# Turning V as 32x32 squares on VectorE, storing it unsplit, and splitting each chunk as it comes back

## The chip, the cores and the metric

The kernel runs on one core of one Trainium2 chip. The metric is the device time of one execution in microseconds, as the median of several executions. Each core has a matrix engine (TensorE, PE in the profile), VectorE (DVE), ScalarE (ACT), GpSimd (POOL) and a queue for DMAs (SyncE, SP). Each engine runs its own instructions in program order, and they meet at semaphores.

## The reference, cut to what matters

One layer works on 2048 tokens of 1024 channels. `x @ w_in` makes all projections; four branches (attention, pooling, a gated recurrence, attention to a memory) are gated, multiplied by `w_branch`, summed, multiplied by `w_out` and normalised. The change lies in the first branch, causal "stick-breaking" attention with 4 heads of 128:

```python
z = jnp.einsum('bhqd,bhnkd->bhqnk', q_blk, k_pre) * scale
log_1m = jnp.where(valid, jax.nn.log_sigmoid(-z), 0.0)
within = jnp.einsum('bhqnk,kj->bhqnj', log_1m, suffix)
later = lax.cumsum(totals, axis=3, reverse=True) - totals
w = jnp.where(valid, jnp.exp(jax.nn.log_sigmoid(z) + within + later[..., None]), 0.0)
o = jnp.einsum('bhqnk,bhnkd->bhqd', w.astype(v.dtype), v_pre)
```

The weight of a key is sigmoid(z) times the product of (1 - sigmoid(z)) over all later keys. So the kernel goes through the keys backwards, with a running product.

## The kernel before, in words

**Precision.** Products are in float32r, as three matmuls: each operand is split into a hi part (a copy rounded to float32r) and a lo part (the difference), and hi·hi + hi·lo + lo·hi is summed (`pass3`, lines 823 to 825).

**Stages.** The tokens are worked in two halves of 1024 (T). In each half `w_in` is applied in 36 pairs of column tiles. A pair is 14 pieces of 6 matmuls of 512 columns (`piece`); sums of blocks on the other engines save one of eight products. The first 8 pairs make Q, K, V and the gate of the four heads. The two pairs of head h+1, and for the last head the first pairs of the merge, are laid as filling between the steps of head h's attention.

**Attention.** For one head, `STEPS` lists steps (chunk c of 512 queries, chunk k of 512 keys, block j of 128 queries): 12 steps a head in the first half and 28 in the second, four to a group with one (c, k). Every engine loops over the same step number s, up to `ns + TAIL`:

- TensorE in step s: `scores(s)` (three matmuls into bank ZZ), then, where s >= 7 and s % 4 == 3, the first half of a group's `values` (W times V), then half pieces of filling, then, where s % 4 == 0, the second half of `values`, and last the transposes `turned(s - TURN)` of the weights of an earlier step, from REST into PSUM (line 949).
- ScalarE in step s: `turned_hi(s - 4)`, the hi copy of turned weights (L1380), then `shares(s)`: two sigmoids of the scores, KEEP (L1366) and SHARE (L1371), then its part of the filling.
- VectorE: `remainder(s - 1)`, a scan of KEEP into REST (L1901), the mask on diagonal steps (L1890), `turned_lo(s - 4)` (L1914) and filling (L1746, L1784).
- GpSimd: `weights(s - 1)`, REST times SHARE in place (L2390), then filling (L2333, L2341, L2320).

In step s = 4i + 7 TensorE starts the values of group i. They read the tile VC, which holds one group's V, hi and lo, in a single buffer.

**How V gets there.** The projection leaves V with channels on partitions. At pieces 10 and 12 of each head's second pair, `turn` lets TensorE transpose it, four 128x128 blocks at a time into a PSUM bank of the projection (L890). ScalarE copies the hi part out (L1277), VectorE subtracts the lo part (L1755), and SyncE stores both to DRAM (`pk_v`, L498). For each group `load_v` reads hi and lo back into VC with one DMA (L518), after the last group's values are done with it.

REST has four slots, one per block j; TURN is 3, so the transposes of step s's weights stand at the end of step s + 3. The first block of the next key chunk takes its start value from the slot of four steps ago.

Of the kernel before, what the change touches and what calls it, by code (L numbers as in the profile page):

```python
# [11 lines left out]
P = 128  # L12
# [70 lines left out]
TURN, TAIL = 3, 5  # L83
# [29 lines left out]
def first_step(half, h):  # L113
    return half * HEADS * NS[0] + h * NS[half]

# [60 lines left out]
def build(nc, xt, xrow, memt, w8, w4, wgate, wpool, prm, cst, ln_g, ln_b, out):  # L176
    with ExitStack() as ctx:
# [24 lines left out]
        B = R + 48.03125  # L202
# [23 lines left out]
        REST = at("REST", R + 32, [BLOCKS, C + 2])  # L226
        WTH = at("WTH", R + 40.03125, [2, BLOCKS, HALF], F32R)
        KC = [at(f"KC{i}", R + 48.03125 + 4 * i, [2, C], F32R) for i in range(2)]
        KEEP = at("KEEP", R + 56.03125, [2, C + 2])
        WTL = at("WTL", R + 60.0625, [2, BLOCKS, HALF], F32R)  # L230
        VC = at("VC", R + 68.0625, [BLOCKS, 2, P], F32R)
# [20 lines left out]
        LR_ = [at(f"LR{i}", R + k, [T]) for i, k in enumerate((28, 8, 52.0625))]  # L252
# [3 lines left out]
        LG = [at(f"LG{i}", R + 52.0625 + 4 * i, [T]) for i in range(2)]  # L256
        LA, LT = at("LA", R + 60.0625, [T]), at("LT", R + 64.0625, [T])
# [38 lines left out]
        pk_v = nc.dram_tensor("pk_v", (HEADS, P, SEQ // P, 2, P), F32).ap()  # L296
# [33 lines left out]
        v_kept = [sem("v_hi_kept"), sem("v_lo_kept")]  # L330
# [3 lines left out]
        v_tr, v_hi, v_blk = sem("v_tr"), sem("v_hi"), sem("v_blk")  # L334
# [122 lines left out]
        def _(sp):  # L457
# [35 lines left out]
            def keep_values(g):  # L493
                half, h = g // PAIRS, g % PAIRS // 2
                hh = half * HEADS + h
                for part, of in ((1, places(half, STL)[1]), (0, places(half, STL)[2])):
                    sp.wait_ge(v_blk, 2 * hh + 2)
                    sp.dma_start(pk_v[h, :, half * TB:(half + 1) * TB, part, :],  # L498
                                 of[:].bitcast(F32).rearrange("p (b m) -> p b m", m=P)).then_inc(v_kept[part], 16)
# [9 lines left out]
            def load_v(half, h, i):  # L509

                n, k = first_group(half, h) + i, STEPS[half][BLOCKS * i][1]
                if i == 0:
                    for kept in v_kept:
                        sp.wait_ge(kept, 16 * (half * HEADS + h + 1))
                    if h == 0:
                        wait_if(sp, o_out[1], 16 * 3 * half)
# [24 lines left out]
            def attention(half, h):  # L541
                ns, fill = NS[half], beside(half, h)
                for g, i in fill[:filled(half, h, -1)]:
                    piece(g, i)
                for s in range(ns + TAIL + 1):
                    if s == ns + 1 and h + 1 == HEADS:
                        sp.wait_ge(z_done, S_END[half])
                        for k in range(2):
                            sp.wait_ge(y_kept, 16 * 2 * (half + 1))
                            sp.dma_start(Y[k][:], pk_y[k]).then_inc(y_back, 16)  # L550
                        load_b(half, 0, 0)
                    if s == 1 and h in (1, 2):
                        sp.wait_ge(y_f, y_count(half, 0, h))
                        sp.dma_start(pk_y[h - 1], Y[h + 1][:]).then_inc(y_kept, 16)
                    if s == 1:
                        load_v(half, h, 0)
                    elif BLOCKS < s <= ns and s % BLOCKS == 0:
                        load_v(half, h, s // BLOCKS - 1)
                    if BLOCKS <= s and s % BLOCKS == 0 and s + BLOCKS < ns:
                        load_k(half, h, s // BLOCKS + 1)  # L560
                    if s in (ns, ns + 1) and h + 1 < HEADS:
                        load_k(half, h + 1, s - ns)
                    if s:
                        for g, i in fill[filled(half, h, s - 2):filled(half, h, s - 1)]:
                            piece(g, i)
# [253 lines left out]
        def _(pe):  # L819
# [16 lines left out]
            def piece(g, i, ks=(0, 1)):  # L836
# [9 lines left out]
                elif i == 0:  # L846
                    pe.wait_ge(a_lo, g + 1)
                    wait_if(pe, ad_done, 4 * (g - 1) + 2)
                    if 2 <= l <= 2 * HEADS and l % 2 == 0:
                        pe.wait_ge(v_blk, 2 * (half * HEADS + l // 2))  # L850
# [30 lines left out]
            def turn(g, part):  # L881

                hh = g // PAIRS * HEADS + g % PAIRS // 2
                v, c = places(g // PAIRS, ST)[2], J[(g + 1) % 2]
                if part:
                    pe.wait_ge(v_blk, 2 * hh + 1)
                else:
                    pe.wait_ge(ad_done, 4 * g + 2)
                for j in range(4):
                    mm = nc.tensor.transpose(c[:, j * P:(j + 1) * P], v[:, (4 * part + j) * P:(4 * part + j + 1) * P],  # L890
                                             IDENT[:])
                mm.then_inc(v_tr, 1)
# [47 lines left out]
            def turned(half, h, s):  # L940

                gs = first_step(half, h) + s
                c, k, j, a, diag, end = STEPS[half][s]
                pe.wait_ge(w_done, gs + 1)
                wait_if(pe, wt_lo, gs - 1)
                n = C - a
                for b in range(n // P):
                    w = REST[:, j, n - P * (b + 1):n - P * b]
                    mm = nc.tensor.transpose(TB_[gs % 2][:, b * P:(b + 1) * P], w, IDENT[:])  # L949
                mm.then_inc(wt_done, 1)  # L950

            def values(half, h, i):
# [6 lines left out]
                pe.wait_ge(v_in, 16 * (n + 1))  # L959
# [182 lines left out]
        def _(act):  # L1142
# [32 lines left out]
            def room(g, p):  # L1175
# [3 lines left out]
                if kind == "head":  # L1179
# [3 lines left out]
                    if i % 2 == 0 and p:  # L1183
                        wait_if(act, v_kept[1], 16 * hh)
                    elif i % 2 == 0 and i:
                        act.wait_ge(sil, half * NB * KB + i // 2)
                    elif i % 2 and p:
                        act.wait_ge(q_kept, 16 * (hh + 1))
                    elif i % 2:
                        wait_if(act, v_kept[0], 16 * hh)  # L1190
                elif kind == "merge" and i >= 2:
                    gates_read(half, n, 2 * i + p - 4)
                elif kind == "merge" and n == 0:
                    if i == 0:
# [3 lines left out]
                        elif half or not p:  # L1198
                            act.wait_ge(k_kept, 32 * HEADS * (half + 1))
                            act.wait_ge(v_kept[1], 16 * HEADS * (half + 1))  # L1200
                        else:
                            act.wait_ge(v_kept[0], 16 * HEADS * (half + 1))
                    elif p:
                        act.wait_ge(w_done, S_END[half])
                    elif half:
                        act.wait_ge(v_kept[0], 16 * HEADS * (half + 1))
# [38 lines left out]
            def piece(g, i):  # L1245
# [24 lines left out]
                if g % PAIRS < 2 * HEADS and g % 2 and i in (10, 12):  # L1270
                    values_hi(g, 0 if i == 10 else 1)

            def values_hi(g, part):

                hh = g // PAIRS * HEADS + g % PAIRS // 2
                act.wait_ge(v_tr, 2 * hh + part + 1)
                nc.scalar.copy(places(g // PAIRS, STL)[2][:, part * C:(part + 1) * C], J[(g + 1) % 2][:]).then_inc(v_hi, 1)  # L1277
# [121 lines left out]
            def attention(half, h):  # L1399
# [8 lines left out]
                for s in range(ns + TAIL + 1):  # L1408
                    if 0 <= s - TURN - 1 < ns:
                        turned_hi(half, h, s - TURN - 1)  # L1410
# [280 lines left out]
        def _(dve):  # L1691
# [56 lines left out]
            def turned(g, part):  # L1748

                hh = g // PAIRS * HEADS + g % PAIRS // 2  # L1750
                t = slice(part * C, (part + 1) * C)
                dve.wait_ge(v_hi, 2 * hh + part + 1)
                dve.wait_ge(k_kept, 32 * (hh + 1))
                hi, lo = places(g // PAIRS, STL)[2], places(g // PAIRS, STL)[1]
                V_.tensor_tensor(lo[:, t], J[(g + 1) % 2][:], hi[:, t].bitcast(F32),  # L1755
                                 ALU.subtract).then_inc(v_blk, 1)
# [30 lines left out]
            def piece(g, i):  # L1787
# [13 lines left out]
                if l < 2 * HEADS and l % 2 and i in (10, 12):  # L1801
                    turned(g, 0 if i == 10 else 1)
# [89 lines left out]
            def remainder(half, h, s):  # L1892
# [4 lines left out]
                n, before = C - a, C - STEPS[half][s - BLOCKS][3]  # L1897
# [3 lines left out]
                V_.tensor_tensor_scan(REST[:, j, 0:n + 1], KEEP[:, gs % 2, 0:n + 1], ZB[gs % 2][:, 0:1].broadcast_to([P, n + 1]),  # L1901
                                      1.0 if diag else REST[:, j, before:before + 1], ALU.mult, ALU.bypass
# [25 lines left out]
            def attention(half, h):  # L1928
# [9 lines left out]
                for s in range(ns + TAIL + 1):  # L1938
# [7 lines left out]
                    if 0 <= s - TURN - 1 < ns:  # L1946
                        turned_lo(half, h, s - TURN - 1)
# [365 lines left out]
        def _(pool):  # L2313
# [69 lines left out]
            def weights(half, h, s):  # L2383
# [5 lines left out]
                w = REST[:, j, 0:n]  # L2389
# [167 lines left out]
```

## Time and profile before

| | |
|---|---|
| median of 3 runs | 2293.91 us (2293.49 to 2294.52) |
| the profiled execution's own time | 2293.96 us |
| its span in the trace | 2292.2 us |
| TensorE matmul busy | 2279.5 us, 99% |
| VectorE, ScalarE, GpSimd busy | 1444.4, 1060.2, 1224.3 us (63%, 46%, 53%) |
| granted TensorE clock | 0.999 of full speed |
| DMA | 297.84 MB, 130 GB/s over the span |

The span runs from the first to the last instruction of the program that was profiled; 1.8 us of the execution lie outside it. Matmuls overlap in the pipeline, so the time of one is read as the distance from its start to the next one's start, not as its duration. The attention of the four heads lies at about 75 to 290 us in the first half and 1150 to 1480 us in the second.

### The profile page before, as it was taken

What the parts mean: (1) busy time and instruction counts of PE and PEld (TensorE: products, weight loads), DVE (VectorE), ACT (ScalarE), POOL (GpSimd) and SP (SyncE); (2) the same over time, 40 slices, a digit from 0 to 9 for tenths busy, and PEclk for the clock granted to TensorE, in tenths of its full rate; (3) what the DMA queues carried; (4) which work ended last, traced back from release to release, by engine and by line L of the source; (5) the groups of instructions that cost most, each with busy time, mean ns of one, the idle gap of its engine ahead of it and who ended that gap; (6) DMA issues with size and microseconds to landing.
All of it is one profiled execution on the core that took longest, in us unless ns stands there. A gap on an engine that the chain in (4) does not pass through costs nothing.

```text
span 2292.2 us, 29991 instructions
## 1 busy us (share of the span) xinstructions
PE 2279.5 (99%) x10824; PEld 1886.8 (82%) x10824; DVE 1444.4 (63%) x1658; ACT 1060.2 (46%) x1627; POOL 1224.3 (53%) x847
## 2 busy tenths in 40 slices
PE   9999999999999999999999999999999999999998
PEld 6888888888878888888888888888888778888887
DVE  7565542764496478568877777733854585486476
ACT  5555542343385255332576676632342583355220
POOL 1666643865456355435476566644863556456341
PEclk9999999999999999999999999999999999999999
DMA  6544422123334345373344543322133334354442
GB/s 234 187 159 158 139 83 97 55 83 129 113 104 133 134 124 148 105 284 138 108 159 139 165 156 124 125 92 78 56 120 124 92 103 134 130 156 132 152 161 83
DMA packets 114419, 297.84 MB, mean 130 GB/s; under 512 B 11232, under 2 KB 41056, under 8 KB 113248
## 3 DMA queue, kind: packets, MB, share of 16 engines
q1 hardware_dynamic: 112544, 290.68, 38.6%
q10 hardware_dynamic: 1728, 5.24, 0.7%
q8 instruction: 87, 1.43, 0.3%
q14 instruction: 60, 0.49, 0.1%
HBM read 216.19 MB, written 71.30 MB: 125 GB/s over the span
## 4 chain that ended last, share of the span: by engine, by line
PE 97%; DVE 1%; DMA 1%; issue 0%; DVEq 0%
PE J L823 21%; PE J L825 21%; PE J L824 21%; PE ZZ L995 8%; PE AO L995 8%; PE ZZ L825 2%; PE ZZ L824 2%; PE ZZ L823 2%; PE AO L825 2%; PE AO L824 2%; PE AO L823 2%; PE AO L949 1%; PE JX L949 1%; PE ZZ L1030 1%; PE JX L825 1%; PE JX L823 1%
## 5 line engine op out<-in xcount | busy, mean ns | idle before, releaser
L2341 POOL TENSOR_TENSOR WLS<-SR,WHS 128x512 fp32r<-128x512 f32 x264 | 414.3, 1588 | 110.1 <-ACT WHS L1161 102.5
L823 PE MATMUL J<-XBH,WHS 128*128 128x512 f32 x1152 | 452.3, 393 | 0.0
L825 PE MATMUL J<-XBH,WLS 128*128 128x512 f32 x1152 | 449.1, 390 | 0.0
L824 PE MATMUL J<-XBL,WHS 128*128 128x512 f32 x1152 | 448.9, 390 | 0.0
L823 PE MATMUL J<-XBH,WH 128*128 128x512 f32 x864 | 340.3, 394 | 0.4 <-DVE WL L1764 0.2
L825 PE MATMUL J<-XBH,WL 128*128 128x512 f32 x864 | 337.0, 390 | 0.0
L824 PE MATMUL J<-XBL,WH 128*128 128x512 f32 x864 | 336.8, 390 | 0.0
L825 PEld LDWEIGHTS J<-XBH,WLS 128*128 128x128 f32 x1152 | 216.2, 188 | 46.0
L824 PEld LDWEIGHTS J<-XBL,WHS 128*128 128x128 f32 x1152 | 216.4, 188 | 43.6 <-issue 0.2
L823 PEld LDWEIGHTS J<-XBH,WHS 128*128 128x128 f32 x1152 | 216.4, 188 | 43.5 <-issue 0.2
L2333 POOL TENSOR_TENSOR SR<-RAW 128x512 f32<-128x512 f32 x71 | 100.6, 1417 | 269.8 <-DMA RAW<-w 230.8
L1746 DVE TENSOR_TENSOR ST<-J,ST 128x512 f32<-128x512 f32 x160 | 109.5, 685 | 209.1 <-PE J L825 162.2
L2390 POOL TENSOR_TENSOR REST<-REST,SHARE 128x512 f32<-128x512 f32 (+3 forms) x160 | 165.6, 1037 | 119.7 <-DVE REST L1901 116.1
L2407 POOL TENSOR_TENSOR BL<-BRAW,BH 128x512 fp32r<-128x512 f32 x64 | 89.3, 1401 | 220.2 <-ACT BH L1429 220.0
L823 PEld LDWEIGHTS J<-XBH,WH 128*128 128x128 f32 x864 | 162.3, 188 | 40.1 <-issue 7.3
L1161 ACT CAST WHS<-SR 128x1024 fp32r<-128x1024 f32 x144 | 151.3, 1051 | 93.5 <-POOL SR L2333 92.4
L825 PEld LDWEIGHTS J<-XBH,WL 128*128 128x128 f32 x864 | 162.2, 188 | 34.8
L824 PEld LDWEIGHTS J<-XBL,WH 128*128 128x128 f32 x864 | 162.3, 188 | 31.8 <-issue 0.2
L2333 POOL TENSOR_TENSOR SR<-SR,RAW 128x512 f32<-128x512 f32 x71 | 105.6, 1488 | 120.4 <-PE J L825 118.4
L1243 ACT COPY ST<-J 128x512 f32<-128x512 f32 x160 | 93.8, 590 | 125.1 <-PE J L825 122.4
L1901 DVE TENSOR_TENSOR_SCAN REST<-KEEP,REST,ZZ 128x513 f32<-128x513 f32 x96 | 122.8, 1279 | 25.5 <-ACT SHARE L1371 24.6
L2333 POOL TENSOR_TENSOR SR<-RAW,SR 128x512 f32<-128x512 f32 x71 | 102.3, 1441 | 51.3 <-PE J L825 50.3
(305 smaller groups left out, 4753.3 us busy)
## 6 DMA issues: line engine op xcount, KB each, us to landing
RAW<-w SPq DMA_DIRECT2D x144, 512.0 KB, 3.7
pk_m<-MB SPq DMA_DIRECT2D x56, 512.0 KB, 5.0
MB<-pk_m SPq DMA_DIRECT2D x48, 512.0 KB, 3.9
KC<-pk_k SPq DMA_DIRECT2D x40, 512.0 KB, 5.4
VC<-pk_v SPq DMA_DIRECT2D x40, 512.0 KB, 4.4
BRAW<-w SPq DMA_DIRECT2D x64, 256.0 KB, 5.0
XRAW<-xt SPq DMA_DIRECT2D x8, 1024.0 KB, 12.6
pk_v<-STL SPq DMA_DIRECT2D x16, 512.0 KB, 5.0
```

The lines of the kernel that those rows point to most:

```text
L823: nc.tensor.matmul(to, wh, xh, start=first, stop=True, skip_group_check=True)
L824: nc.tensor.matmul(to, wh, xl, start=False, stop=True, skip_group_check=True)
L825: return nc.tensor.matmul(to, wl, xh, start=False, stop=True, skip_group_check=True)
L995: mm = nc.tensor.matmul(BR[p][c][:], w[p][:, k, :], y[k][:, c * C:(c + 1) * C], start=(k == 0 and m == 0), stop=(k == KB - 1 and m == 2))
L1161: nc.scalar.copy(WHS[:, k, :], SR[:, k, :]).then_inc(w_hi, 1)
L1243: nc.scalar.copy(dest(g)[p][:, c * C:(c + 1) * C], J[(g + bank) % 2][:]).then_inc(cp_done, 1)
L1746: V_.tensor_tensor(d, bank[:], d, ALU.add).then_inc(ad_done, 1)
L1901: V_.tensor_tensor_scan(REST[:, j, 0:n + 1], KEEP[:, gs % 2, 0:n + 1], ZB[gs % 2][:, 0:1].broadcast_to([P, n + 1]), 1.0 if diag else REST[ ...
L2333: G_.tensor_tensor(SR[:, 4 * j:4 * j + 4], a, b, op).then_inc(s_raw, 1)
L2341: low = G_.tensor_tensor(WLS[:, k, :], SR[:, k, :], WHS[:, k, :].bitcast(F32), ALU.subtract)
L2390: G_.tensor_tensor(w, w, SHARE[gs % 2][:, 0:n], ALU.mult).then_inc(w_done, 1)
L2407: G_.tensor_tensor(BL[f % 2][:], BRAW[f % 2][:], BH[f % 2][:].bitcast(F32), ALU.subtract).then_inc(b_lo, 1)
```

## The change

VectorE now turns V itself, with its 32x32 transpose, two instructions a head at piece 10, from the V tile into the place of K; TensorE's transposes (`turn`), ScalarE's hi copies and VectorE's subtractions of V in the filling go. V is stored once, unsplit, with one DMA in place of two. For each group four DMAs of 32 partitions each gather the squares into a new tile VRAW, with the four key blocks interleaved (element m of block b at 4m + b). ScalarE copies the hi part out of it into VC (`values_hi`), GpSimd subtracts the lo part (`values_lo`), both in their step s = 4i + 6 and both reading every fourth float. TensorE's values wait for `vc_lo`. To make room for VRAW, REST has three slots of 5 + 512 + 1 floats in place of four of 514, used in turn by step number, and TURN is 2 in place of 3.

```diff
-TURN, TAIL = 3, 5
+TURN, SPLIT, TAIL = 2, 4, 5
+SLOTS, SHIFTS = 3, 5
-        REST = at("REST", R + 32, [BLOCKS, C + 2])
+        REST = at("REST", R + 32, [SLOTS, SHIFTS + C + 1])
+        VRAW = at("VRAW", R + 38.09375, [C])
 # SyncE
             def keep_values(g):
...
+                sp.wait_ge(v_tr, NC * (hh + 1))
+                sp.dma_start(pk_v[h, :, half * TB:(half + 1) * TB, :],
+                             places(half, ST)[1][:].rearrange("p (b m) -> p b m", m=P)).then_inc(v_kept, 16)
 # load_v
-                wait_if(sp, pv_done, 2 * n)
-                sp.dma_start(VC[:].bitcast(F32), pk_v[h, :, BLOCKS * (k ^ 1):BLOCKS * (k ^ 1) + BLOCKS]).then_inc(v_in, 16)
+                wait_if(sp, vc_lo, n)
+                for q in range(GROUPS):
+                    rows = pk_v[h, :, GROUPS * (k ^ 1) + q].rearrange("(i x) m -> x i m", i=GROUPS)
+                    to = VRAW[SQUARE * q:SQUARE * (q + 1)].rearrange("x (i m) -> x i m", i=GROUPS)
+                    sp.dma_start(to, rows).then_inc(v_in, 16)
...
-                    elif BLOCKS < s <= ns and s % BLOCKS == 0:
-                        load_v(half, h, s // BLOCKS - 1)
+                    elif BLOCKS < s < ns and s % BLOCKS == BLOCKS - 1:
+                        load_v(half, h, s // BLOCKS)
 # TensorE
-                if l < 2 * HEADS and l % 2 and i in (10, 12):
-                    turn(g, 0 if i == 10 else 1)
...
-                pe.wait_ge(v_in, 16 * (n + 1))
+                pe.wait_ge(vc_lo, n + 1)
 # ScalarE
+            def values_hi(half, h, i):
+                n = first_group(half, h) + i
+                act.wait_ge(v_in, 16 * GROUPS * (n + 1))
+                wait_if(act, pv_done, 2 * n)
+                if h == 0 and i == 0:
+                    wait_if(act, o_out[1], 16 * 3 * half)
+                nc.scalar.copy(VC[:, :, 0, :], VRAW.rearrange("p (m b) -> p b m", b=BLOCKS)).then_inc(vc_hi, 1)
...
                     if s < ns:
                         shares(half, h, s)
+                    if TAIL < s < ns + BLOCKS and s % BLOCKS == 2:
+                        values_hi(half, h, s // BLOCKS - 1)
 # VectorE, at piece 10
+            def turn_values(g):
+                hh = g // PAIRS * HEADS + g % PAIRS // 2
+                dve.wait_ge(ad_done, 4 * g + 2)
+                dve.wait_ge(k_kept, 32 * (hh + 1))
+                _, to, v = places(g // PAIRS, ST)
+                for c in range(NC):
+                    t = slice(c * C, (c + 1) * C)
+                    V_.transpose(to[:, t].rearrange("p (q x b) -> p b q x", q=GROUPS, b=BLOCKS),
+                                 v[:, t].rearrange("p (b n) -> p b n", b=BLOCKS)).then_inc(v_tr, 1)
 # remainder
-                wait_if(dve, wt_done, gs - BLOCKS + 1)
+                wait_if(dve, wt_done, gs - SLOTS + 1)
 # GpSimd
+            def values_lo(half, h, i):
+                n = first_group(half, h) + i
+                pool.wait_ge(vc_hi, n + 1)
+                G_.tensor_tensor(VC[:, :, 1, :], VRAW.rearrange("p (m b) -> p b m", b=BLOCKS), VC[:, :, 0, :].bitcast(F32),
+                                 ALU.subtract).then_inc(vc_lo, 1)
...
                     if 1 <= s <= ns:
                         weights(half, h, s - 1)
+                    if TAIL < s < ns + BLOCKS and s % BLOCKS == 2:
+                        values_lo(half, h, s // BLOCKS - 1)
```

## Rows read from the trace of the kernel before

**Rows 1.** The page: busy time, and the chain that ended last.
```profile
PE 2279.5 (99%) x10824; PEld 1886.8 (82%) x10824; DVE 1444.4 (63%) x1658; ACT 1060.2 (46%) x1627; POOL 1224.3 (53%) x847
...
PE 97%; DVE 1%; DMA 1%; issue 0%; DVEq 0%
```
**Rows 2.** Waits, TensorE's own: in total, times, longest (us).
```profile
PE AO L823 <- DMA VC<-pk_v: 0.8, 3, 0.3
PEld J L890 <- DVE STL L1755: 1.0, 3, 0.3
```
**Rows 3.** Timeline of TensorE at a turn of V: start, length (us), engine, line, operation.
```profile
68.23 0.40 PE L825 MATMUL J<-XBH,WLS 128*128 128x512 f32 x1
68.47 0.60 PE L890 MATMUL J<-IDENT,ST 128*128 128x128 f32 x4
68.82 0.48 PE L823 MATMUL J<-XBH,WHS 128*128 128x512 f32 x1
69.14 0.39 PE L824 MATMUL J<-XBL,WHS 128*128 128x512 f32 x1
69.37 0.40 PE L825 MATMUL J<-XBH,WLS 128*128 128x512 f32 x1
```
**Rows 4.** Timeline of step 26 of the second head, second half (s = 4i + 6).
```profile
1294.73 0.39 PE L825 MATMUL ZZ<-KC,QL 128*128 128x512 f32 x1
1295.16 0.60 ACT L1366 ACTIVATE KEEP<-ZZ 128x512 f32<-128x512 f32 x1
1295.66 0.59 ACT L1371 ACTIVATE SHARE<-ZZ 128x512 f32<-128x512 f32 x1
1296.14 0.59 ACT L1243 COPY ST<-J 128x512 f32<-128x512 f32 x1
1297.25 0.19 PEld L823 LDWEIGHTS AO<-WTH,VC 128*128 128x128 f32 x1
1297.48 0.28 PE L823 MATMUL AO<-WTH,VC 128*128 128x256 f32 x1
```
**Rows 5.** Timeline: ScalarE releases GpSimd.
```profile
1303.27 1.05 ACT L1161 CAST WHS<-SR 128x1024 fp32r<-128x1024 f32 x1
1304.40 1.29 POOL L2341 TENSOR_TENSOR WLS<-SR,WHS 128x512 fp32r<-128x512 f32 x1 [1.84 <-ACT WHS L1161]
```
**Rows 6.** Timeline, the place with the longest window (first head, first half, s = 10).
```profile
109.40 0.63 ACT L1371 ACTIVATE SHARE<-ZZ 128x512 f32<-128x512 f32 x1
112.02 0.19 PEld L823 LDWEIGHTS AO<-WTH,VC 128*128 128x128 f32 x1
```
**Rows 7.** Timeline, a place where GpSimd is late (second half, first head, s = 6).
```profile
1158.50 1.30 POOL L2320 TENSOR_TENSOR WL<-RAW,WH 128x512 fp32r<-128x512 f32 x1
1159.39 0.39 PE L825 MATMUL ZZ<-KC,QL 128*128 128x512 f32 x1
1159.74 2.35 POOL L2390 TENSOR_TENSOR REST<-REST,SHARE 128x512 f32<-128x512 f32 x2
```
**Rows 8.** Lines: durations ns min/median/max; L2341 from 1150 to 1480 us.
```profile
L2390 POOL TENSOR_TENSOR REST<-REST,SHARE x160: 452/1094/1306, 81.2 to 1467.5; 128x512 f32<-128x512 f32 x112, 128x128 f32<-128x128 f32 x16, 128x256 f32<-128x256 f32 x16, 128x384 f32<-128x384 f32 x16
L2341 POOL TENSOR_TENSOR WLS<-SR,WHS x28: 1287/1292/1756, 1166.6 to 1466.2; 128x512 fp32r<-128x512 f32 x28
L1161 ACT CAST WHS<-SR x144: 1035/1050/1084, 13.4 to 2157.5; 128x1024 fp32r<-128x1024 f32 x144
L2125 DVE STREAM_TRANSPOSE PB<-PR x12: 1245/1245/1247, 818.3 to 2055.9; 128x1024 f32<-128x1024 f32 x12
```
**Rows 9.** The page's group of L2341, all stages: its mean.
```profile
L2341 POOL TENSOR_TENSOR WLS<-SR,WHS 128x512 fp32r<-128x512 f32 x264 | 414.3, 1588 | 110.1 <-ACT WHS L1161 102.5
```
**Rows 10.** Timeline: a transpose of weights, and the lower part two steps behind it.
```profile
1462.19 0.59 PEld L949 LDWEIGHTS AO<-IDENT,REST 128*128 128x128 f32 x4
1462.71 0.66 DVE L1914 TENSOR_TENSOR WTL<-JX,WTH 128x512 fp32r<-128x512 f32 x1
```
**Rows 11.** Waits: of ScalarE and VectorE on turned weights, and of SyncE's queue.
```profile
ACT WTH L1380 <- PE AO L949: 62.3, 57, 2.6
DVE WTL L1914 <- ACT WTH L1380: 54.4, 46, 2.5
SPq L518 <- PE AO L825: 232.8, 32, 13.0
```

More of the change, by code:

```diff
@@ L114, in first_step, with rest_place @@
     return half * HEADS * NS[0] + h * NS[half]
+def rest_place(half, s):
+    c, k, j, a, diag, end = STEPS[half][s]
+    return SHIFTS - (s - (ENDS[half][c - 1] + 1 if c else 0)) // SLOTS + a
 def first_group(half, h):
@@ L225, in build @@
         SHARE = [at(f"SHARE{i}", R + 28 + 2 * i, [C]) for i in range(2)]
-        REST = at("REST", R + 32, [BLOCKS, C + 2])
[L227 to L231, printed above, removed]
+        REST = at("REST", R + 32, [SLOTS, SHIFTS + C + 1])
+        VRAW = at("VRAW", R + 38.09375, [C])
+        WTH = at("WTH", R + 40.09375, [2, BLOCKS, HALF], F32R)
+        KC = [at(f"KC{i}", R + 48.09375 + 4 * i, [2, C], F32R) for i in range(2)]
+        KEEP = at("KEEP", R + 56.09375, [2, C + 2])
+        WTL = at("WTL", R + 60.125, [2, BLOCKS, HALF], F32R)
+        VC = at("VC", R + 68.125, [BLOCKS, 2, P], F32R)
         GT = [ST[1], ST[2], ST[0], at("GT3", R + 28, [T])]
@@ L255, in build @@
         LU_ = [at(f"LU{i}", R + k, [4 + T]) for i, k in enumerate((48.03125, 40))]
-        LG = [at(f"LG{i}", R + 52.0625 + 4 * i, [T]) for i in range(2)]
-        LA, LT = at("LA", R + 60.0625, [T]), at("LT", R + 64.0625, [T])
+        LG = [at(f"LG{i}", R + 52.125 + 4 * i, [T]) for i in range(2)]
+        LA, LT = at("LA", R + 60.125, [T]), at("LT", R + 64.125, [T])
         WGR = at("WGR", R + 68.25, [P])
@@ L512, in load_v @@
                 if i == 0:
[L513 to L516, printed above, removed]
-                wait_if(sp, pv_done, 2 * n)
-                sp.dma_start(VC[:].bitcast(F32), pk_v[h, :, BLOCKS * (k ^ 1):BLOCKS * (k ^ 1) + BLOCKS]).then_inc(v_in, 16)
+                    sp.wait_ge(v_kept, 16 * (half * HEADS + h + 1))
+                wait_if(sp, vc_lo, n)
[3 more added lines that the diff above has]
+                    sp.dma_start(to, rows).then_inc(v_in, 16)
             def piece(g, i):
@@ L877, in piece @@
                     mm.then_inc(pr_done, 1)
-                if l < 2 * HEADS and l % 2 and i in (10, 12):
-                    turn(g, 0 if i == 10 else 1)
[L881 to L892, printed above, removed]
             def pair(g, inside={}, first=0):
@@ L945, in turned @@
                 wait_if(pe, wt_lo, gs - 1)
-                n = C - a
+                n, first = C - a, rest_place(half, s)
                 for b in range(n // P):
-                    w = REST[:, j, n - P * (b + 1):n - P * b]
+                    w = REST[:, gs % SLOTS, first + n - P * (b + 1):first + n - P * b]
                     mm = nc.tensor.transpose(TB_[gs % 2][:, b * P:(b + 1) * P], w, IDENT[:])
@@ L1205, in room @@
                     elif half:
-                        act.wait_ge(v_kept[0], 16 * HEADS * (half + 1))
+                        act.wait_ge(v_tr, NC * HEADS * (half + 1))
                     else:
@@ L1408, in attention @@
                 for s in range(ns + TAIL + 1):
-                    if 0 <= s - TURN - 1 < ns:
-                        turned_hi(half, h, s - TURN - 1)
+                    if 0 <= s - SPLIT < ns:
+                        turned_hi(half, h, s - SPLIT)
                     if s < ns:
                         shares(half, h, s)
+                    if TAIL < s < ns + BLOCKS and s % BLOCKS == 2:
+                        values_hi(half, h, s // BLOCKS - 1)
                     if s == ns and h + 1 < HEADS:
@@ L1800, in piece @@
                     rest_of_sums(g + 1, False)
-                if l < 2 * HEADS and l % 2 and i in (10, 12):
-                    turned(g, 0 if i == 10 else 1)
+                if l < 2 * HEADS and l % 2 and i == 10:
+                    turn_values(g)
             def pair(g, after={}, first=0):
@@ L1896, in remainder @@
                 dve.wait_ge(share_done, gs + 1)
-                n, before = C - a, C - STEPS[half][s - BLOCKS][3]
+                n, before = C - a, rest_place(half, s - BLOCKS) + C - STEPS[half][s - BLOCKS][3]
                 if h == 0 and s < 2:
                     dve.wait_ge(ones_made, half + 1)
-                wait_if(dve, wt_done, gs - BLOCKS + 1)
-                V_.tensor_tensor_scan(REST[:, j, 0:n + 1], KEEP[:, gs % 2, 0:n + 1], ZB[gs % 2][:, 0:1].broadcast_to([P, n + 1]),
-                                      1.0 if diag else REST[:, j, before:before + 1], ALU.mult, ALU.bypass
+                wait_if(dve, wt_done, gs - SLOTS + 1)
+                first = rest_place(half, s)
+                V_.tensor_tensor_scan(REST[:, gs % SLOTS, first:first + n + 1], KEEP[:, gs % 2, 0:n + 1],
+                                      ZB[gs % 2][:, 0:1].broadcast_to([P, n + 1]),
+                                      1.0 if diag else REST[:, (gs - BLOCKS) % SLOTS, before:before + 1], ALU.mult, ALU.bypass
                                       ).then_inc(scan_done, 1)
@@ L1945, in attention @@
                         piece(*pieces.pop(0))
-                    if 0 <= s - TURN - 1 < ns:
-                        turned_lo(half, h, s - TURN - 1)
+                    if 0 <= s - SPLIT < ns:
+                        turned_lo(half, h, s - SPLIT)
                     if s == ENDS[half][0] + TAIL + 1:
@@ L2388, in weights @@
                 pool.wait_ge(scan_done, gs + 1)
-                w = REST[:, j, 0:n]
+                first = rest_place(half, s)
+                w = REST[:, gs % SLOTS, first:first + n]
                 G_.tensor_tensor(w, w, SHARE[gs % 2][:, 0:n], ALU.mult).then_inc(w_done, 1)
+            def values_lo(half, h, i):
[3 more added lines that the diff above has]
+                                 ALU.subtract).then_inc(vc_lo, 1)
             def attention(half, h):
```

36 lines of the change are left out of this document (9 added, 27 removed).

## The prediction

> **What bounds the kernel now.** I read the page first: TensorE is busy 99% of the span and 97% of the chain that ended last [rows 1]. Then its waits: in the whole execution it waits 0.8 us for V's DMA in three places, 1.0 us for V's lower part in three, and hardly for anything else after the start [rows 2]. So two things count: matrix work that leaves, and any new wait of TensorE. Work moved between the other engines costs nothing as long as TensorE never sees it. Last I read the timeline of the attention steps, where the new chain has to fit [rows 4 to 7].
>
> **What leaves TensorE.** 16 turns of V of four transposes. From the matmul before a turn (start 68.23) to the second after it (69.14) are 0.91 us; two matmuls take 2 x 0.23 of that, 69.14 to 69.37 being one of them, so a turn costs 0.45 us [rows 3]. 16 x 0.45 = 7.3 us. With the waits of rows 2, 0.8 + 1.0, the gain is 9.1 us. It is real: it lies on the bound engine with nothing beside it.
>
> **What VectorE, ScalarE and SyncE take on in the filling.** VectorE's 16 transposes of 128x512 replace 16 subtractions of V. The trace has the transpose at 128x1024, 1.25 us [rows 8], so by half the columns at least 0.62 us and at most the 1.25 us, against 0.68 us for the subtraction. They come back to back instead of two pieces apart, up to 2.5 us at once, but V is needed only some six steps later. ScalarE loses 16 copies. The store becomes one DMA for two. I cost this at nothing; the cover is the head's first six steps.
>
> **The load.** It becomes four DMAs, 120 more issues on SyncE in all, and moves from behind the last values of a group to step 4i + 3, where SyncE waits for the lower part of the group before. SyncE now sits 232.8 us in this line waiting for TensorE [rows 11], so the queue has room for the issues, and the data has three steps of over 2.5 us to land in. Zero; if it came late, ScalarE's copy, with the sigmoids queued behind it, would stand and the stall below would grow.
>
> **The new chain into the values.** Here is the cost. In step s = 4i + 6 ScalarE copies the hi part behind `shares(s)`, GpSimd then subtracts, and TensorE needs the result straight behind `scores(s + 1)`. `shares(s)` cannot start before `scores(s)` is done. So the chain from one product of scores to the next has to hold two sigmoids, a copy and a subtraction. In the trace [rows 4]: the last scores matmul starts 1294.73, KEEP 1295.16, SHARE 1295.66; the copy that follows SHARE there runs from 1296.14 to 1296.73. A hi copy of V, of the same size, would stand in its place. GpSimd starts 0.08 us behind a copy that ends at 1304.32 [rows 5], here at 1296.81. With a subtraction of 1.5 us it ends at 1298.31, and 0.06 us later (an estimate, a little under that 0.08) TensorE may load V: 1298.37. In the trace it loads V at 1297.25. TensorE stands 1.12 us. Matmuls behind it can't pass.
>
> **The length of the subtraction.** No row has one that reads every fourth float. The nearest from below is the product of two dense tiles, 1.09 us; the same subtraction on dense tiles is 1.29 us at the median and 1.76 at most in this stage [rows 8], and its mean over all stages is 1.59 us [rows 9]. I take 1.5 us, between median and maximum of the stage and near that mean, because a strided read will hardly be faster than a dense one. The hi copy I take as the dense 0.59 us, and as its upper end the 1.05 us of the ScalarE copy twice as long [rows 8].
>
> **The Trainium skill on this.** "GPSIMD Engine Reference", Performance pitfalls for Q7 kernels, says that a read of SBUF whose step is over 8 bytes costs about half as much again per element; here the step is 16 bytes. No row of this trace can confirm it; by that rule the 1.29 us would be 1.94 us (an estimate), and the sum would be the one of the first rival.
>
> **Counting the places.** A head has 3 groups in the first half and 7 in the second, 40 in all. The last group of a head is free: its copy comes at step ns + 2, with no scores before it and whole steps of filling to cover it; that is 8 groups. For the other 32 I read the same instants from the timeline:
>
> - 13 as above: 1.11 to 1.15 us each, 14.5 in sum.
> - 6 where the window is a little shorter or the sigmoids end later: 1.27 to 1.29, 7.7 in sum.
> - 10 between 1.36 and 3.10, 19.3 in sum. In seven of these GpSimd itself is late: in rows 7 a lower part and the product `weights(s - 1)` stand before it, the first of the two products (1.1 us each) ends at 1160.85, and V would be loaded at 1159.39. Eight of the ten are in a fourth head.
> - 3 in the first half with a long window: SHARE ends 110.03, so the copy at 110.51 and the subtraction at 112.09, against a load at 112.02 [rows 6]: 0.13 each, 0.4 in sum.
>
> In sum 41.9 us. It repeats fully: every group starts anew from its own scores, so a stand of TensorE doesn't buy the next group time. With 1.09 us the same sum is 29.6, with 1.29 it is 35.4, with 1.76 it is 50.3.
>
> **TURN 2, three slots.** The transposes of a step's weights move one step forward. By the timeline GpSimd's product would come after that place in 3 of 152 pairs of steps, 1.1 us in all. VectorE's lower part, which frees the PSUM bank, ends after it in 41 of 136, 17.5 us in all; the largest is 1.24 us, where the transposes start at 1462.19 and the lower part ends at 1463.37 [rows 10]. But today this lower part is late because ScalarE waits for those same transposes (62.3 us, and 49.9 more on the other bank) and VectorE for ScalarE (54.4) [rows 11], and they now come a step earlier. Bounds 0 and 18.6; I take 2, near the lower one, since the stands above also let VectorE catch up. The scan's new wait, for the transposes of three steps before, is met: they stand ahead of the scores it needs anyway.
>
> **Sum.** 2294.0 (the execution of the trace; 0.05 above the median of 2293.9) - 9.1 + 41.9 + 2.0 = 2328.8, so 2329 us.
>
> **Rivals.**
>
> 1. *The strided read is dear.* If the subtraction takes half as long again as the dense median, 1.94 us, the 32 places sum to 56.0: 2294 - 9.1 + 56.0 + 2 = 2343 us. For it: each float read lies 16 bytes from the last, which no row covers, and dense ones have already taken 1.76 us. Against: only one of its two inputs is strided. 22%. The Trainium skill's rule named above leads to this rival.
> 2. *A second wait per group.* `values_lo` keeps GpSimd waiting for ScalarE and delays `weights(s)`, which TensorE now wants a step sooner; in a fourth head that slack is under 0.6 us in several steps. With the whole 18.6 of the TURN bounds: 2294 - 9.1 + 41.9 + 18.6 = 2345 us. Against: TensorE's own stand, just before, gives most of that back. 10%.
> 3. *The split is in time (the other side).* If ScalarE's copy and GpSimd's subtraction together took under 0.85 us (1297.25 less 1296.25, less 0.14 for the two handovers), no place of the 13 would stall, and what is left is the gain: 2294 - 9.1 = 2285 us. For it: 11 of 40 groups have nearly no stall even now. Against: the shortest pair of rows is 0.48 + 1.09. 6%, and 3% for about equal, where few places stall.
>
> **How the numbers follow.** The forecast, the stall with a subtraction of 1.1 to 1.76 us, holds 59%; its own range is 2294 - 9.1 + 29.6 = 2314 to 2294 - 9.1 + 50.3 + 2 = 2337. The range given reaches from 2308, for handovers and copy some tenths shorter than read, up to 2352, which takes in both slower rivals and part of a hi copy of 1.05 us (29 places x 0.46 = 13 us more). Left out are rival 3 and the tail above. A change of 0.2% (4.6 us) is what a measurement can tell from none. Faster 0.06, same 0.03, slower 0.91.
>
> **What would show it.** Line 890 gone, 64 fewer matrix instructions. TensorE's waits: about 30 on the GpSimd subtraction, mean 1.3 us, none in the last group of a head and three near 0.1. The subtraction's length tells the forecast from rival 1, waits on `weights` or the lower part show rival 2. The forecast is wrong if TensorE waits for the split in under ten places, or if its waits sum to less than the 9 us it gained.

## The result and the profile after

The changed kernel takes 2356.14 us in the median (2355.29 to 2360.1, 4 runs), the kernel before 2294.16 us beside it (2293.49 to 2294.52, 4 runs). The ratio is 1.0274, 95% interval 1.0261 to 1.0286. The change is slower by 62 us; the forecast was 35 us, 2329 us with a range up to 2352. The direction and the mechanism were right; the price was not, and the measured time lies above the range.

The page of the profile after, which answers to [rows 1]: busy time, and the chain that ended last.

```profile
PE 2290.5 (97%) x10760; PEld 1883.6 (80%) x10760; DVE 1451.2 (62%) x1658; ACT 1082.8 (46%) x1651; POOL 1290.1 (55%) x887
...
PE 41%; DVE 3%; POOL 2%; issue 2%; ACT 2%; DMA 0%; SPq 0%; DVEq 0%; POOLq 0%; ACTq 0%
```

The 64 transposes are gone, but TensorE's share fell. (The shares of this chain add up to about half of the span, so the view does not follow it all the way, and its 41% is not a busy share; what matters is that GpSimd, ScalarE and VectorE are now on it.) TensorE's waits after, answering to [rows 2]: total, times, longest (us).

```profile
PE AO L831 <- POOL VC L2394: 35.7, 26, 2.5
PE AO L831 <- DVE WTL L1911: 10.9, 8, 1.4
PE AO L899 <- DMA MW<-w: 4.8, 1, 4.8
PE JX L940 <- DVE WTL L1911: 2.8, 7, 0.6
PE ZZ L831 <- DVE REST L1897: 1.0, 1, 1.0
```

The first line is the predicted wait. The second is the same one for the most part: values wait for two semaphores, and the profile names VectorE's lower part at 8 places, although V's weight load comes 0.11 to 0.12 us behind the end of GpSimd's subtraction in all 32 places. The two lines hold 34 places, two more than predicted: the values of the last group of the fourth head, once in each half, wait for the split too, 1.0 us (at 295.4 us) and 0.35 us (at 1531.2). A step of the second head, second half, timeline after (start, length, us), against [rows 4]:

```profile
1316.98 0.39 PE L833 MATMUL ZZ<-KC,QL 128*128 128x512 f32 x1
...
1317.41 0.60 ACT L1358 ACTIVATE KEEP<-ZZ 128x512 f32<-128x512 f32 x1 [1.15 <-PE ZZ L833]
...
1317.91 0.59 ACT L1363 ACTIVATE SHARE<-ZZ 128x512 f32<-128x512 f32 x1
...
1318.38 1.14 ACT L1269 CAST VC<-VRAW 128x512 fp32r<-128x512 f32 x1
...
1319.60 1.52 POOL L2394 TENSOR_TENSOR VC<-VRAW,VC 128x512 fp32r<-128x512 f32 x1 [1.25 <-ACT VC L1269]
...
1321.23 0.19 PEld L831 LDWEIGHTS AO<-WTH,VC 128*128 128x128 f32 x1 [1.77 <-DVE WTL L1911]
1321.27 0.36 PE L831 MATMUL AO<-WTH,VC 128*128 128x256 f32 x1 [1.37 <-POOL VC L2394]
1321.46 0.28 PE L832 MATMUL AO<-WTL,VC 128*128 128x256 f32 x1
```

From the last scores matmul to V's weight load are 4.25 us; before, 1294.73 to 1297.25, 2.52 us [rows 4]. Link by link the chain is the predicted one, and one link is off: the copy takes 1.14 us, not 0.59. The new instructions, from the views of their lines, with min/median/max in ns (CAST is the copy that rounds to float32r):

```profile
L1269 ACT CAST VC<-VRAW x40: 1098/1129/1192, 96.2 to 1528.3; 128x512 fp32r<-128x512 f32 x40
...
L2394 POOL TENSOR_TENSOR VC<-VRAW,VC x40: 1516/1526/1573, 97.4 to 1529.5; 128x512 fp32r<-128x512 f32 x40
...
L1750 DVE STREAM_TRANSPOSE ST<-ST x16: 1074/1098/1119, 69.9 to 1437.4; 128x512 f32<-128x512 f32 x16
```

One thing that [rows 1] to [rows 11] never show: inside the attention TensorE's clock now falls. Stretches of the timeline after, busy us of PE, PEld, DVE, ACT, POOL, then the granted clock:

```profile
1205.00:1210.00 5.00, 3.27 (x19) 2.30 (x17) 3.01 (x3) 3.93 (x8) 2.65 (x2) 1.00 0.00 0
1210.00:1215.00 5.00, 4.70 (x19) 4.10 (x20) 4.23 (x4) 2.34 (x5) 4.61 (x4) 0.66 0.51 174
```

After a stretch in which TensorE was busy 3.27 of 5 us, standing for V, the clock goes from 2.4 to 1.2 GHz for part of the next 5 us: 0.34 x 5 = 1.7 us lost. This happens four times in the attention (near 160, 1212, 1297 and 1487 us), 3.4 us at the lower level each time and so 6.8 us lost in all; in the kernel before, not once there.

### The profile page after: what moved, and what is told of

Read it like the earlier page. It is cut to its first block, busy times and chain, and to the rows that moved or that the text cites. A ratio compares the mean times of both kernels' runs of the same rounds, so it can differ in the third digit from the quotient of the medians.

```text
span 2353.4 us, 30069 instructions
## 1 busy us (share of the span) xinstructions
PE 2290.5 (97%) x10760; PEld 1883.6 (80%) x10760; DVE 1451.2 (62%) x1658; ACT 1082.8 (46%) x1651; POOL 1290.1 (55%) x887
## 4 chain that ended last, share of the span: by engine, by line
PE 41%; DVE 3%; POOL 2%; issue 2%; ACT 2%; DMA 0%; SPq 0%; DVEq 0%; POOLq 0%; ACTq 0%
PE J L831 8%; PE J L832 8%; PE J L833 8%; PE AO L986 4%; PE ZZ L986 4%; PE AO L831 1%; PE AO L833 1%; PE AO L832 1%; DVE REST L1897 1%; POOL VC L2394 1%; PE ZZ L833 1%; PE ZZ L831 1%; PE ZZ L832 1%; POOL REST L2388 1%; ACT SHARE L1363 1%
## 5 line engine op out<-in xcount | busy, mean ns | idle before, releaser
L2330 POOL TENSOR_TENSOR SR<-SR,RAW 128x512 f32<-128x512 f32 x71 | 104.7, 1475 | 120.1 <-PE J L833 117.6
L1897 DVE TENSOR_TENSOR_SCAN REST<-KEEP,REST,ZZ 128x513 f32<-128x513 f32 x96 | 122.9, 1280 | 61.3 <-ACT SHARE L1363 59.2
L1358 ACT ACTIVATE KEEP<-ZZ 128x512 f32<-128x512 f32 (+3 forms) x160 | 86.4, 540 | 139.5 <-PE ZZ L833 124.2
```

The costliest lines, as they stand in the source:

```text
L1897: V_.tensor_tensor_scan(REST[:, gs % SLOTS, first:first + n + 1], KEEP[:, gs % 2, 0:n + 1], ZB[gs % 2][:, 0:1].broadcast_to([P, n + 1]), 1 ...
L2330: G_.tensor_tensor(SR[:, 4 * j:4 * j + 4], a, b, op).then_inc(s_raw, 1)
```

## The experiments

Ratios are to the kernel before, run beside each. Where the text says "trace", one profiled run of that kernel is meant. A stand is time for which TensorE is held back: the distance from the start of one matmul to the start of the next, less the usual distance for that pair of shapes in the trace of before.

**e1, both reads dense.** In `values_hi` and `values_lo`:

```diff
-VRAW.rearrange("p (m b) -> p b m", b=BLOCKS)
+VRAW.rearrange("p (b m) -> p b m", b=BLOCKS)
```

> The changed kernel with both reads of VRAW dense (the copy and the subtraction read 512 floats in a row, so the key blocks get the wrong rows: the computation of the attention output is left wrong, work and sizes are the same). Theory A (the copy took 1.13 us instead of 0.59, and the subtraction 1.53 instead of 1.29, because of the step of 16 bytes, and each of the 32 places pays for both): the copy falls to 0.59, the subtraction to 1.29, TensorE's wait ahead of the values falls from 1.53 to about 0.8 us per place, and the time from 2356 by 32 x 0.75 = 24 us to about 2332. Rival B (the copy is long because of something else, such as the four DMAs or the engine's place in the step): both durations stay and the time stays at 2356. Rival C (the time lost beyond the forecast is in TURN 2): durations fall but the time only by the forecast's share, under 12 us.

Measured: 2326.56 us, ratio 1.0141 (1.0125 to 1.0158), 29.6 us less than the change. The two instructions in its trace:

```profile
L1269 ACT CAST VC<-VRAW x40: 617/621/664, 96.3 to 1502.6; 128x512 fp32r<-128x512 f32 x40
...
L2394 POOL TENSOR_TENSOR VC<-VRAW,VC x40: 1267/1286/1614, 97.0 to 1503.3; 128x512 fp32r<-128x512 f32 x40
```

Theory A holds, B and C fall. The step of 16 bytes makes ScalarE's copy 1.8 times and GpSimd's subtraction 1.19 times as long. From scores to V's load, the 32 places sum to 117.6 us instead of 139.2, 21.6 us less. The stands ahead of the values fall from 50.9 us to 29.4, 0.92 us a place. There is one clock fall in place of four (near 1170 us, where the change had none), which gives 5.1 us more; that was in no expectation, and with it the time lies 5 us under the 2332 of theory A.

**e10, ScalarE's read alone dense.**

> The changed kernel with ScalarE's copy alone reading dense (wrong rows of V, so the attention output is left wrong), GpSimd's subtraction as in the change. Of the 29.6 us between the change and e1 theory A gives the copy 0.51 / 0.75 and the subtraction 0.24 / 0.75: 2356 - 20 = 2336 (2333 to 2340). Rival H (the subtraction's part is larger, since it also delays GpSimd's products): 2341 or more.

Measured: 2336.24 us, ratio 1.018 (1.0166 to 1.0194). Of e1's 29.6 us, 2356.14 - 2336.24 = 19.9 us are the copy's and 2336.24 - 2326.56 = 9.7 us the subtraction's. In the traces the stands ahead of the values go from 50.9 us to 37.3 and 29.4, 13.6 us by the copy and 7.9 by the subtraction, and the clock falls from four to one with the copy alone, the 5.1 us. So the copy's 19.9 us are stands and clock together. Rival H falls.

**e2, the copy ahead of the sigmoids.** In ScalarE's loop, `values_hi` is called before `shares(half, h, s)` of the same step.

> The changed kernel with ScalarE's copy of V ahead of the two sigmoids of the same step instead of behind them; nothing else. Theory A (the stall comes from the chain scores, two sigmoids, copy, subtraction, values within one step): the copy no longer waits for the scores, TensorE's wait ahead of the values falls from 50.9 us in sum to under 10, and the time to 2305 (2296 to 2315). Rival B (the lengths of copy and subtraction are what counts, wherever they stand, since they keep ScalarE and GpSimd busy): the sigmoids come later by the copy's 1.1 us, and the time stays over 2335.

Measured: 2318.4 us, ratio 1.0106 (1.0091 to 1.0121), 38 us less. Direction as A, but 3 us over its interval, and the stands did not fall under 10 us as A had it. The trace shows what ends last now:

```profile
1262.78 1.15 ACT L1269 CAST VC<-VRAW 128x512 fp32r<-128x512 f32 x1
...
1263.89 1.30 POOL L2388 TENSOR_TENSOR REST<-REST,SHARE 128x512 f32<-128x512 f32 x1 [1.06 <-DVE REST L1897]
...
1264.11 0.39 PE L833 MATMUL ZZ<-KC,QL 128*128 128x512 f32 x1
...
1265.14 1.57 POOL L2394 TENSOR_TENSOR VC<-VRAW,VC 128x512 fp32r<-128x512 f32 x1
...
1266.83 0.19 PEld L831 LDWEIGHTS AO<-WTH,VC 128*128 128x128 f32 x1 [0.24 <-issue]
```

The copy is done at 1263.93, before the last matmul of this step's scores starts; the subtraction waits for GpSimd's own product `weights(s - 1)`, till 1265.2, and TensorE for the subtraction. This product ends behind the copy at 28 of the 32 places. 18.9 us of stands remain in 27 places, against 50.9 in 32, and here too one clock fall is left of four: 32.0 + 5.1 us of the 38. The chain through one step's scores was the larger part of the loss; the product in front of the subtraction is the next link.

**e3, split and load one step earlier.**

```diff
-                    if TAIL < s < ns + BLOCKS and s % BLOCKS == 2:
+                    if TAIL <= s < ns + BLOCKS and s % BLOCKS == 1:
-                    elif BLOCKS < s < ns and s % BLOCKS == BLOCKS - 1:
+                    elif BLOCKS < s < ns and s % BLOCKS == 2:
```

> The changed kernel with copy and subtraction one step earlier (s = 4i + 5) and the load of V one step earlier (s = 4i + 2). Theory A: no place waits for the split any more; what is left is the gain of the transposes (7.3 us and the 1.8 us of waits) against the waits that TURN 2 brings (about 6 us ahead of the transposes in the changed kernel's trace, 1 us at scores): 2291 (2286 to 2300). Rival C (TURN 2 and three slots cost much more once the stalls no longer give VectorE and GpSimd time to catch up): 2305 or more.

Measured: 2309.47 us, ratio 1.0068 (1.0053 to 1.0083). No place waits for the split, as A said, but the time is rival C's. TensorE's waits in its trace:

```profile
PE JX L940 <- DVE WTL L1911: 5.4, 9, 1.4
...
PE AO L940 <- POOL REST L2388: 3.9, 4, 1.8
PE AO L940 <- DVE WTL L1911: 2.2, 4, 0.6
PE ZZ L831 <- DVE REST L1897: 1.7, 1, 1.7
```

They are the second wait of the prediction's rival 2: ahead of the transposes, 19.4 us by the starts of matmuls, on VectorE's lower part and on GpSimd's product.

**e4, TURN 2 and three slots on the kernel before.** The edit is the change's own REST, SLOTS, SHIFTS, TURN and SPLIT, and nothing of V.

> The kernel before with REST in three slots and TURN 2 alone (V as before, by TensorE's transposes). Theory A (TURN 2 is a small term, the forecast's 2 us or a few more, as 6.2 us ahead of the transposes in the changed kernel's trace): 2299 (2296 to 2304). Rival C (it is a large term, up to the 18.6 us of the upper bound or over): 2308 or more.

Measured: 2305.87 us, ratio 1.0052 (1.0037 to 1.0067): 11.9 us slower. Between the two expectations: six times the 2 us I took, two thirds of the upper bound of 18.6. In its trace 10.2 us stand ahead of the transposes, and TensorE waits 2.1 us for V's DMA instead of 0.8. One of the larger stands, 0.8 us ahead of the transposes at 1283.00:

```profile
1279.46 1.62 DVE L1785 TENSOR_TENSOR WL<-RAW,WH 128x512 fp32r<-128x512 f32 x1
...
1280.64 0.62 ACT L1388 CAST WTH<-AO 128x512 fp32r<-128x512 f32 x1
...
1281.00 1.27 DVE L1910 TENSOR_TENSOR_SCAN REST<-KEEP,REST,ZZ 128x513 f32<-128x513 f32 x1
...
1282.20 0.66 DVE L1923 TENSOR_TENSOR WTL<-AO,WTH 128x512 fp32r<-128x512 f32 x1
...
1283.00 0.63 PE L957 MATMUL AO<-IDENT,REST 128*128 128x128 f32 x4 [0.66 <-DVE WTL L1923]
```

The hi part (WTH) is there at 1281.26, but VectorE is in its filling till 1281.08 and in the scan till 1282.27, and subtracts the lower part (WTL) only then; TensorE's transposes need that PSUM bank.

**e7, three slots alone, TURN 3.**

```diff
-TURN, SPLIT, TAIL = 2, 4, 5
+TURN, SPLIT, TAIL = 3, 4, 5
```

> The kernel before with REST in three slots and TURN left at 3; with e4 it separates the place of the transposes from the number of slots. Theory C: TensorE hardly waits, 2295 (2293 to 2299). Rival E: the slots are what costs in e4, 2303 or more.

Measured: 2297.42 us, ratio 1.0014 (1.0005 to 1.0023), 3.3 us slower. Theory C: most of e4's loss is the place of the transposes, not the number of slots.

**e6, e3 with TURN 3.** The same edit on e3.

> The kernel of e3 (split one step early) with TURN back at 3 and still three slots: TensorE turns a step's weights at the end of step s + 3 as before the change, but VectorE's scan of step s now has to wait for the transposes of step s - 3, which end only with step s. Theory C (what e3 and e4 lose is TensorE waiting, at the place one step early, for GpSimd's product and VectorE's lower part): those waits fall from 19.4 us to under 3, the scan starts about 0.7 us later per step without TensorE seeing it, and the time falls from 2309 to 2292 (2286 to 2297). Rival E (with three slots the scan's wait only passes the loss on to the scores and products): 2305 or more.

Measured: 2295.64 us, ratio 1.0005 (0.9996 to 1.0014), 13.8 us less than e3. Theory C again. What is left is mostly the scan, which now waits for its slot; at three places 0.8 us of waiting for the split is back. TensorE's waits in the trace:

```profile
PE ZZ L831 <- DVE REST L1897: 4.7, 5, 1.3
...
PE AO L831 <- POOL VC L2394: 0.8, 3, 0.3
```

**e11, e6 with the transposes straight behind the scores.** In TensorE's loop, `turned(half, h, s - TURN)` moves from the end of the step to behind `scores(half, h, s)`.

> The kernel of e6 with TensorE's transposes of weights straight behind the scores of step s (still those of step s - 3) instead of at the end of the step, so that VectorE's scan gets its slot before the filling. Theory C: e6's 6 us of waits for the scan go (5 places), the products are ready at this place (they had at least 1.5 us of slack at the end of step s in the kernel before, and the filling between is 1.4 us), so 2289 (2286 to 2292), faster than both kernels. Rival I (the product is late at the earlier place in the fourth heads): 2294 or more.

Measured: 2294.57 us, ratio 1.0002 (0.9993 to 1.0011): no change from before, rival I. The first three heads of the first half run 0.8 us faster each than before and the middle heads of the second half 0.5 and 0.9, but the first head of the second half loses 2.5 us, and from the last head on 2.0 are lost. The waits have only moved:

```profile
PE ZZ L831 <- DVE REST L1897: 2.8, 4, 1.7
PE AO L940 <- POOL REST L2388: 1.6, 2, 1.2
```

**e9, the changed kernel whole with TURN 3.**

> The changed kernel whole, with TURN back at 3 on its three slots. Theory A plus C (the stall ahead of the values and the waits of TURN 2 are separate terms that add up): the first stays at about 50 us, the second, 14 us between e3 and e6, goes: 2342 (2337 to 2347). Rival G (TensorE's stand for the split already hides most of TURN 2's waits, as rival 2 of the prediction had it): 2351 or more.

Measured: 2382.57 us, ratio 1.0389 (1.0373 to 1.0405): 26 us slower than the change, where both theories had expected the same or less. TensorE's waits in its trace:

```profile
PE AO L831 <- POOL VC L2394: 59.2, 34, 3.1
PE AO L831 <- DVE WTL L1911: 8.2, 6, 1.4
```

Three things grew. With TURN 3 on three slots the scan waits for later transposes; the product `weights(s - 1)` ends behind the copy at 12 of 32 places instead of 2, and scores to V's load sum to 150.5 us instead of 139.2, 11.3 us more. Second, the last group of every head now waits for the split as well: ahead of its values 12.4 us stand in the eight places, against 1.4 in the change. ScalarE's copy there follows a hi copy of turned weights that waits for transposes which TURN 3 puts one step later, as in the trace of e9:

```profile
311.96 0.59 ACT L1372 CAST WTH<-JX 128x512 fp32r<-128x512 f32 x1 [0.74 <-PE JX L940]
312.44 1.13 ACT L1269 CAST VC<-VRAW 128x512 fp32r<-128x512 f32 x1
```

Third, the clock: 30.6 us at the lower level in the attention instead of 13.6, 8.5 us lost (the mean over the span falls from 0.997 to 0.993). Less the 5.2 us ahead of the transposes, which are gone, this makes 25.6 us, where the two spans differ by 24.8. TURN 2 is a loss beside a split that is in time (e3 against e6) and a gain beside one that isn't: the terms don't add.

**e12, e3 with dense reads.**

> The kernel of e3 (TURN 2, split one step early) with both reads of VRAW dense (wrong rows of V, so the attention output is left wrong). It tells whether the length of copy and subtraction still counts once the chain into the values has slack. Theory J (the 40 subtractions on GpSimd push its products of weights, and TURN 2 wants those a step sooner, which is why e3's waits ahead of the transposes, 19.4 us, are 9 us over e4's): the subtraction falls by 0.27 us and the copy by 0.5, the waits to about 15 us, the time from 2309 to 2304 (2301 to 2307). Rival K (off the path the lengths don't count, and e3's waits have another cause): 2308 or more.

Measured: 2302.07 us, ratio 1.0035 (1.0023 to 1.0048), 7.4 us less than e3. Theory J: ahead of the transposes stand 12.3 us instead of 19.4. Even off the chain of V the lengths count, as long as TURN 2 leaves GpSimd's products little slack.

**e5, the kernel before without TensorE's transposes of V.**

```diff
-                for j in range(4):
-                    mm = nc.tensor.transpose(...)
-                mm.then_inc(v_tr, 1)
+                pe.nop().then_inc(v_tr, 1)
```

> The kernel before without TensorE's 64 transposes of V alone: ScalarE and VectorE still split the bank in the same places, so V holds other numbers (the transposition of V is left out). Theory A (the gain term of the prediction, 16 x 0.45 = 7.3 us, is right, with up to 1.0 us of waits that may stay): 2286.5 us, between 2285.5 and 2287.5. Rival D (the transposes lay beside something else, so the gain was less): 2290 or more.

Measured: 2289.45 us (2287.76 to 2290.74, 11 runs), ratio 0.9979 (0.997 to 0.9988): 4.6 us, between A and D. In the trace each of the first three heads is 0.92 us shorter (two turns of 0.45), but the first head of the second half is 1.2 us longer. New waits give some of the gain back, the largest 1.5 us once for a scan, 0.8 us once in the memory branch and 0.8 us once for V's lower part:

```profile
PE ZZ L823 <- DVE REST L1898: 1.5, 1, 1.5
PE AO L823 <- DVE PTL L2137: 0.8, 1, 0.8
PE J L823 <- DVE STL L1752: 0.8, 1, 0.8
```

**e8, VC interleaved.** Copy and subtraction write as they read; TensorE loads `VC[:, 0, :, BLOCKS - 1 - b]`.

> The kernel of e3 with V's tile VC kept interleaved (element m of block b at 4m + b), so that copy and subtraction read and write dense and TensorE's weight loads of V read every fourth float instead. Theory A plus C (the lengths of copy and subtraction count through GpSimd's time, 0.27 us per group, once the chain is off the path): copy 0.62, subtraction 1.29 as in e1, TensorE's wait for GpSimd's product falls, 2304 (2300 to 2308), if the strided weight loads stay hidden. Rival F (strided weight loads are longer than the 0.12 us between two matmuls of 256 columns): each of 864 loads of V costs, 2340 or more at double length.

Measured: 2387.88 us, ratio 1.0407 (1.0392 to 1.0421), rival F: 78 us more than e3. The weight loads of V, min/median/max:

```profile
L831 PEld LDWEIGHTS AO<-WTH,VC x288: 307/330/332, 97.5 to 1567.3; 128*128 128x128 f32 x144
```

They took 0.19 us before. In e3 two matmuls of V with 256 columns start 0.118 us apart, here 0.233; all matmuls of V together take 191.1 us instead of 109.0.

## Why the prediction was wrong

- **TensorE's gain, 9.1 us.** The transposes cost what [rows 3] say, 0.9 us a head, but e5 gives 4.6 us in all. Part of the gain turns into waits elsewhere; why just those, the runs don't settle.
- **The mechanism of the stall.** Right in place and shape, and nearly in number: the 32 places, and the chain scores, two sigmoids, copy, subtraction, values. e2 and e3 show it by moving a link. "None in the last group of a head" did not quite hold: two places there, both in a fourth head. The load, put at nothing, has a small part in this: in the last group of each head of the first half ScalarE's copy waits for VRAW's DMA, 2.6 us in four places, and only the fourth head's reaches TensorE, in the 1.0 us.
- **The size of the stall, the step that failed.** I said "the hi copy I take as the dense 0.59 us" and kept 1.05 us only as an upper end. It is 1.13 us; e1 and e10 show that the 16-byte step does it. With the copy alone dense (e10) the time is 2336 us, inside the range. The forecast counted how much later V's weight load starts. By that measure the 32 places, from scores to load, went from 81.3 us to 139.2, 57.9 more, where 41.9 + 32 x 0.54 = 59.2 would follow from the longer copy. What TensorE loses is a little less, since its first matmul follows a late load after 0.03 us and not 0.23: the stands ahead of the values sum to 50.9 us (0.7 of which stood there before), and the matmul behind each is 0.08 us late as well, 53.5 in all.
- **The subtraction.** 1.5 us forecast, 1.53 measured. Rival 1's half as long again did not come: e1 has 1.29 dense, so 19% more. The handover to the weight load, estimated at 0.06 us, took 0.12. I had put the doubt on the wrong engine: the strided read was weighed for GpSimd alone, though ScalarE reads the same tile in the same way. The rule of the Trainium skill ("GPSIMD Engine Reference", Performance pitfalls for Q7 kernels: half as much again) is not what this instruction shows, with one of its two inputs strided: 1.53 against 1.29 us. The Trainium skill's page "SBUF — State Buffer", section "Door 1: The DMA port swizzle", in its box on SBUF cachelines, says that full bandwidth needs at least two hits per 16-byte line, and a step of 16 bytes has one. ScalarE's 0.62 and 1.13 us agree with that sentence. The next one in the same box lets fp32 stride up to 4 elements for free, which is this very step, and these two numbers speak against it; so the page by itself would have left the copy's length open, and the doubt belonged into the sum.
- **TURN 2, taken as 2 us.** e4 measures 11.9. The argument for the lower bound was that the transposes come a step earlier, and so the lower part behind them too. That did not hold: the kernel still copies and subtracts turned weights four steps behind (SPLIT is 4), and the lower part comes in VectorE's program order, behind the scan of a later step (the lines under e4). In the change itself only 5.2 us stand ahead of the transposes at full clock. That the stands above let the engines catch up, as the prediction said, fits e3, where those stands are gone and 19.4 us stand ahead of the transposes.
- **What no step had: the clock.** Four stretches at the lower level, 6.8 us.
- **Rival 3's threshold.** It took the copy's start as the end of SHARE, 1296.25, but in [rows 4] the copy starts at 1296.14: the split would be in time below 0.97 us, not 0.85. Measured, copy and subtraction take 1.13 + 1.53 = 2.66 us.
- **The sum by what was measured** (spans, 2353.4 - 2292.2 = 61.2): 53.5 ahead of the values in the 32 places, 1.0 ahead of the last group's in the first half's fourth head, 5.2 ahead of the transposes, 1.2 at scores, 6.8 clock, less 7.3 for the transposes: 60.4.
- **The range.** Its upper end took "part of" the longer copy. The forecast's own upper end of 2337, with the 13 us for a copy of 1.05 us and e4's 12 us for TURN 2 in place of 2, would have reached 2360.

## What to carry to other kernels

Before a tile is laid out, list every engine that reads it and price its stride for each: here an interleaved tile made one copy 1.8 times as long, in the one place where it stood between two matmul groups. A split that needs nothing of the running step should not stand behind work that waits for it; issued one step earlier it is waited for nowhere (e3). And two terms that share an engine's slack can't be measured apart and added: TURN 3 saves 14 us with the split early and costs 26 us with it late.

## What the runs showed of the hardware

- A read of fp32 at a step of 16 bytes, 128x512: ScalarE's copy 1.13 us against 0.62, GpSimd's subtraction with one of two inputs strided 1.53 against 1.29 (the change and e1); TensorE's weight load of 128x128 0.33 against 0.19 (e8).
- VectorE's 32x32 transpose of 128x512 with its writes at a step of 16 bytes takes 1.10 us; the one of 128x1024 with runs of 32 took 1.25 [rows 8].
- With stands of TensorE for V of 0.4 to 2.7 us in 32 places, its clock fell to the lower level four times in the attention, each time at the end of a stand of 2.0 to 2.2 us or up to 1.5 us behind it; in e3, with no stand for V, not once. At five other stands of 2.0 to 2.7 us in the change it did not fall, and in e10 it fell at one of 1.3 us and not at one of 2.6. What decides it stays open. In e9, with 62.2 us of stands in these places instead of 50.9, the mean clock fell to 0.993.
- In the change ScalarE's copy hands over to GpSimd in 0.08 us (1319.52 to 1319.60), GpSimd's subtraction to TensorE's weight load in 0.12 us.
- A matmul whose weight load was held back starts 0.03 us behind the load and delays the next by 0.08 us, not by the 0.23 us by which loads usually run ahead.
